# State-space turns of a two-block transformer kernel: seven GpSimd operations in place of five VectorE operations

## The reference, cut to what matters

```python
dt = jnp.exp(log_step.astype(f32))[:, None]
mag = jnp.exp(lr * dt)
ab_r = mag * jnp.cos(li * dt)
ab_i = mag * jnp.sin(li * dt)
...
_, _, s_r, s_i = lax.associative_scan(_complex_linear_combine, (a_r, a_i, bu_r, bu_i), axis=1)
```

## Time and profile before

| | |
|---|---|
| runs shown, median | 2434.28 us (3 runs, 2433.3 to 2437.17) |
| profiled execution, its own time | 2435.06 us |
| its span | 2433.4 us |
| granted TensorE clock over the span | 0.997 of full |
| PE busy | 2404.1 us |
| DVE, ACT, POOL busy | 1712.9, 1223.4, 527.3 us |

### The profile page before, as it was taken

The page is one execution under the profiler, slowest core; times in us unless marked ns, Lnnn a source line. Parts: engine busy times, 40 slices in busy tenths (PEclk is TensorE's granted clock), DMA queues, the critical chain, the costliest instruction groups (busy, mean ns, idle before and its releaser), DMA issues.

```text
span 2433.4 us, 45170 instructions
## 1 busy us (share of the span) xinstructions
PE 2404.1 (99%) x15288; PEld 2173.7 (89%) x15288; DVE 1712.9 (70%) x2649; ACT 1223.4 (50%) x1838; POOL 527.3 (22%) x1003
## 2 busy tenths in 40 slices
PE   8999999999999999999999999999999999999999
PEld 7888888989999999999999999998888888888888
DVE  8977776668888887678888875666555555555555
ACT  5455454455666665566665444444444444444442
POOL 2310032246767773210011221111000000000000
PEclk9999999999999999999999999999999999999999
DMA  7765566656666665555557876766777677777774
GB/s 243 218 201 198 189 216 209 188 184 202 198 204 209 200 196 179 187 185 196 167 189 245 262 219 223 228 201 179 204 191 191 191 192 190 190 190 192 190 190 147
DMA packets 257100, 485.07 MB, mean 199 GB/s; under 512 B 23688, under 2 KB 171860, under 8 KB 256736
## 3 DMA queue, kind: packets, MB, share of 16 engines
q1 hardware_dynamic: 216064, 415.66, 56.2%
q10 hardware_dynamic: 29632, 35.30, 4.5%
q0 software_dynamic: 11296, 32.68, 4.4%
HBM read 455.20 MB, written 31.08 MB: 200 GB/s over the span
## 4 chain that ended last, share of the span: by engine, by line
PE 85%; DVE 8%; issue 3%; ACT 3%; DMA 0%; ACTq 0%; DVEq 0%; SPq 0%; POOL 0%; POOLq 0%
PE z_ps L2191 14%; PE z_ps L2179 9%; PE z_ps L2181 9%; PE z_ps L2180 9%; PE z_ps L2192 7%; PE z_ps L2590 7%; PE z_ps L2591 7%; PE z_ps L2596 7%; DVE w_lo L1393 3%; ACT w_hi L753 1%; PE o_ps L2234 1%; PE s_ps L2216 1%; PE p_ps L2626 1%; PE o_ps L2626 1%; PE v_ps L2626 1%
## 5 line engine op out<-in xcount | busy, mean ns | idle before, releaser
L1393 DVE TENSOR_TENSOR w_lo<-w_raw,w_hi 128x1024 fp32r<-128x1024 f32 x518 | 638.9, 1262 | 221.4 <-ACT w_hi L753 219.5
L753 ACT ACTIVATE w_hi<-w_raw 128x1024 fp32r<-128x1024 f32 x518 | 529.4, 1050 | 243.1 <-PE z_ps L2192 130.3
L2050 DVE TENSOR_TENSOR w_lo<-w_raw,w_hi 128x1024 fp32r<-128x1024 f32 x262 | 320.8, 1226 | 300.5 <-ACT w_hi L1233 300.2
L2191 PE MATMUL z_ps<-x_both,w_hi 128*128 128x512 f32 x1440 | 517.9, 402 | 6.7 <-DVE w_lo L1393 3.5
L1233 ACT ACTIVATE w_hi<-w_raw 128x1024 fp32r<-128x1024 f32 x262 | 277.9, 1061 | 415.3 <-PE z_ps L2596 267.8
L2179 PE MATMUL z_ps<-x_both,w_hi 128*128 128x256 f32 x1376 | 398.5, 290 | 7.2 <-DVE w_lo L1393 6.5
L2192 PE MATMUL z_ps<-x_both,w_lo 128*128 128x256 f32 x1440 | 404.1, 281 | 0.0
L2181 PE MATMUL z_ps<-x_both,w_lo 128*128 128x256 f32 x1376 | 390.5, 284 | 0.0
L2180 PE MATMUL z_ps<-x_both,w_hi 128*128 128x256 f32 x1376 | 390.4, 284 | 0.0
L2191 PEld LDWEIGHTS z_ps<-x_both,w_hi 128*128 128x128 f32 x1440 | 271.8, 189 | 70.5 <-issue 7.1
L2179 PEld LDWEIGHTS z_ps<-x_both,w_hi 128*128 128x128 f32 x1376 | 265.0, 193 | 11.8 <-issue 10.1
(11 more groups left out here) (464 smaller groups left out, 4183.9 us busy)
## 6 DMA issues: line engine op xcount, KB each, us to landing
w_raw<-in_w SPq DMA_DIRECT2D x624, 512.0 KB, 4.3
w_raw<-in_w SPq DMA_DIRECT2D x160, 256.0 KB, 3.3
w_raw<-in_w SPq DMA_DIRECT2D x80, 384.0 KB, 4.9
w_raw<-in_w SPq DMA_DIRECT2D x80, 128.0 KB, 3.0
tab_d<-arena ACTq DMA_DIRECT2D x32, 256.0 KB, 2.9
res<-tab_d POOLq DMA_DIRECT2D x16, 384.0 KB, 5.6
arena<-tab_d POOLq DMA_DIRECT2D x16, 384.0 KB, 5.8
tab_d<-arena ACTq DMA_DIRECT2D x32, 128.0 KB, 2.5
```

The costliest lines, as they stand in the source:

```text
L753: act.activation(w_hi[:, n % RING, :], w_raw[:, n % RING, :], ACT.Copy).then_inc(w_hi_ready, 1)
L1393: dve.tensor_tensor(w_lo[:, n % RING, :], w_raw[:, n % RING, :], w_hi[:, n % RING, :].bitcast(F32), ALU.subtract).then_inc(w_lo_ready, 1)
L2050: dve.tensor_tensor(w_lo[:, k % RING, :], w_raw[:, k % RING, :], w_hi[:, k % RING, :].bitcast(F32), ALU.subtract).then_inc(w_lo_ready, 1)
L2191: pe.matmul(z[:], wh, both[:, :, kt, :], start=(first and kt == kts[0]), stop=False)
```

## The change

The turns of all 32 tiles are made on GpSimd. The bounded, reduced product is the same. VectorE has an operation that takes two tensors and a scalar at once, and it used that twice; on GpSimd each of the two is written as two operations, so the five become seven, with a wait on `turn_step` in front of each of the last four. The place changes too. VectorE made the even tile's turns behind the evacuation of the gate and the odd tile's ahead of the split for job 3 of the period. GpSimd makes them inside `tile_powers(st)`, behind the second of the three products of the loop, so ahead of the third and the last one. Tile 0's turns come behind the sums of squares of layer 0, behind a wait for the copy of `d_col` on VectorE, which reads a part of the same memory. The first wait of `tile_turns`, for `tab_ready`, goes along with it.

```diff
+            def tile_turns(st):
+                reach(pool, tab_ready, st)
+                f, f_hi, f_lo = (ssm_f[:, i, st:st + 1] for i in range(3))
+                pool.tensor_scalar(turn_k, times_in, f, ROUND, ALU.mult, ALU.add)
+                pool.tensor_scalar(turn_d, times_in, f_hi, None, ALU.mult)
+                pool.tensor_scalar(turns, times_in, f_lo, None, ALU.mult).then_inc(turn_step, 1)
+                pool.wait_ge(turn_step, 4 * st + 2)
+                pool.tensor_scalar(turn_k, turn_k, -ROUND, None, ALU.add).then_inc(turn_step, 1)
+                pool.wait_ge(turn_step, 4 * st + 3)
+                pool.tensor_tensor(turn_d, turn_k, turn_d, ALU.subtract).then_inc(turn_step, 1)
+                pool.wait_ge(turn_step, 4 * st + 4)
+                pool.tensor_tensor(turns, turns, turn_d, ALU.subtract).then_inc(turn_step, 1)
+                pool.wait_ge(turn_step, 4 * st + 5)
+                pool.tensor_scalar(turns, turns, 0.5, -0.5, ALU.min, ALU.max).then_inc(turns_ready, 1)
...
                 for m in range(3):
                     times(x[:, :, m + 1:8 - m:6 - 2 * m, :], x[:, :, m:9 - m:8 - 2 * m, :], xt_t, l_r, l_i, 3 + 3 * m)
+                    if m == 1 and st > 0:
+                        tile_turns(st)
                 times(x[:, :, 4, :], x[:, :, 3, :], xt_t[:, :, 0, :], l_r, l_i, 12)
...
+            pool.wait_ge(t_vec_landed, 16)
+            pool.wait_ge(turn_step, 1)
+            tile_turns(0)
             for st in range(1, ST):
                 tile_powers(st)
...
-                dve.tensor_scalar(turn_k, times_in, f, ROUND, ALU.mult, ALU.add)
-                dve.tensor_scalar(turn_d, times_in, f_hi, None, ALU.mult).then_inc(turn_step, 1)
-                dve.wait_ge(turn_step, 3 * st + 1)
-                dve.scalar_tensor_tensor(out=turn_d, in0=turn_k, scalar=-ROUND, in1=turn_d,
-                                         op0=ALU.add, op1=ALU.subtract).then_inc(turn_step, 1)
-                dve.wait_ge(turn_step, 3 * st + 2)
-                dve.scalar_tensor_tensor(out=turns, in0=times_in, scalar=f_lo, in1=turn_d,
-                                         op0=ALU.mult, op1=ALU.subtract).then_inc(turn_step, 1)
-                dve.wait_ge(turn_step, 3 * st + 3)
-                dve.tensor_scalar(turns, turns, 0.5, -0.5, ALU.min, ALU.max).then_inc(turns_ready, 1)
...
-                if l == 1:
-                    tile_turns(2 * h)
...
-                if l == 1:
-                    tile_turns(2 * h + 1)
```

More of the change, by code:

```diff
@@ L579, in load_c @@
                 pool.dma_start(c_in, ap["ssm_c"][st]).then_inc(c_landed, 16)
+            times_in = t_vec.rearrange("p (k i) -> p k i", i=STEP)[:, :, 0]
+            def tile_turns(st):
[12 more added lines that the diff above has]
+                pool.tensor_scalar(turns, turns, 0.5, -0.5, ALU.min, ALU.max).then_inc(turns_ready, 1)
             XT_STEPS = 15
@@ L1620, in _ @@
                     dve.wait_ge(consts_landed, (7 + STEP) * 16)
-                    chain(dve.tensor_copy(d_col.rearrange("p (c s) -> p s c", s=SPC), d_in))
+                    dve.tensor_copy(d_col.rearrange("p (c s) -> p s c", s=SPC), d_in).then_inc(turn_step, 1)
+                    dve.wait_ge(turn_step, 1)
                     chain(dve.memset(tab_out[:, 2 * P:3 * P], 0.0))
```

## The result

| | before | after |
|---|---|---|
| median of the runs | 2434.99 us (4 runs, 2433.3 to 2437.17) | 2563.98 us (4 runs, 2563.81 to 2566.1) |
| profiled execution, its span | 2433.4 us | 2562.3 us |
| granted TensorE clock over the span | 0.997 | 0.976 |

A forecast was written before the change was run, and what follows sets the result against it. PE, busy 2404.1 of 2433.4 us, was taken to bound the kernel. 15 x (5.7 wait + 2.4 clock) - 2.5 = 119 us on the profiled 2435.06 gave 2554, median 2553 us; range 2495 to 2585.

The forecast's parts named there:

- turns, undisturbed: POOL's seven operations a tile in layer 1, priced at a same-shape product's row: 2.27 us, bounds 1.4 and 3.1.
- a pair of splits in the chain: DVE's pair of splits for job 3's successor falls into POOL's new chain and costs POOL about 1.9 us.
- chain on POOL: From ACT's line 806 to PE's release at odd tiles: turns, third and last products, releases, splits; 7.0 us.
- slack of PE behind line 806: Time from ACT's end of line 806 on the even tile to PE's odd tile: mean 1.28 us, least 0.53.
- wait of PE: PE waits for POOL at the odd tile in fifteen of sixteen periods: 7.0 - 1.28 = 5.7 us each.
- low clock behind it: After each PE wait the granted clock drops; priced at the middle of 3.1 and 1.6 us: 2.4 us.
- start of the layer, once: Shorter 4.40 us PE wait for a split in layer 1's second period, plus 0.5 us elsewhere: -2.5 us.
- the room is there as a sum: POOL in layer 1: 19.2 us busy plus 4.6 added makes 23.8 of a 26.67 us period.
- Undisturbed and full clock: Rival, 12%: POOL interleaves better with DVE's splits and the clock holds; odd-tile wait 3.8 us, +55 us, 2489.
- Dear operations: Rival, 8%: each new POOL operation takes some 0.77 us, turns 5.6 us, wait 9.0; +180 us, 2614.
- The turns fit: Rival, 7%: POOL's chain is shorter than the slack; gain only at the layer's start, -3 to -6 us, 2430.
- hidden altogether: Rival, 3%: the turns fit the slack, with nothing gained at the layer's start either; 2434 us.

The follow-up runs named there:

- the run with one in seven: Changed kernel with turns moved behind the powers' last product and six of the seven operations left out, only the clamp kept: 2431.1 us, 0.9983 of the kernel before.
- the load alone: Kernel before, VectorE still making the turns, plus the seven operations on GpSimd behind each tile's powers from tile 3, into unread memory: 2468.62 us, 1.014.
- two sets of turns: Changed kernel with three small tiles of their own for odd tiles from 3 on, so turns wait for the tile before the last: 2479.34 us, 1.0179.
- The wait alone: Kernel before with only POOL's wait for ACT added at the place of the new turns, VectorE still making them: 2495.66 us, 1.0249.

## Why the prediction was right, and where it was not

**The mechanism holds.** PE waits for POOL at the odd tile of fifteen periods, and not at the even one, once the layer is under way. POOL begins its chain when ACT is through with line 806, since the turns exist once. Two parts of the chain were tried alone: the wait (+60 us without any turns) and the work behind it (1.49 us for a product of 1.52). The third, DVE's splits, is read from two kinds of waits in one run (1.19 against 3.13 us).

**The terms.** As they were put and as they came:

| a period | predicted | measured |
|---|---|---|
| turns, undisturbed | 2.27 us | 2.94 us |
| a pair of splits in the chain | 1.9 | 1.76 |
| chain on POOL | 7.0 | 7.66 |
| slack of PE behind line 806 | 1.28 | 1.39 |
| wait of PE | 5.7 | 6.26 |
| low clock behind it | 2.4 | 35.01 - 26.67 - 6.26 = 2.08 |
| start of the layer, once | -2.5 | +3.8 |

The pair is the mean length of the fifteen blocks of turns in the chain, 4.70 us, less 2.94. The last two rows are what is left over, of a period and of the 128.9 us, so that 15 x (6.26 + 2.08) + 3.8 = 128.9 comes out by itself. Independent readings stand beside them: 2.13 us a wait by the granted clock, 30.8 us more busy time of PE, and at the start PE ready for tile 3 at 580.32 - 6.15 = 574.17 us, 4.05 later than in the kernel before, which began it at 570.12. The forecast's sum was 9.9 us short: 8.4 by the waits and 6.3 by the start of the layer, less 4.8 by a clock term that was too dear. Part of the agreement is thus luck. So is the clock term itself, the middle of two gaps: the windows behind such waits spread from 0.58 to 0.80, and the shorter waits of the run with the turns one product later lost more. The bounds of the range had slips of 0.2 us, too: with turns of 1.4 us the chain adds up to 6.1 and not 5.9 (a wait of 4.8, not 4.6), and with 3.1 it is 7.8 without any further disturbance.

The turns were priced at the row of a product of the same shape, 0.29 us. The sums (lines 593 and 595) take 0.32 and the last operation 0.24, but lines 587 and 591 take 0.38 and the two reads of the times at lines 588 and 589 take 0.51 and 0.53. The input of lines 587 to 589 lies strided in `t_vec` (every fourth value), and a scalar comes from `ssm_f`. The stride alone is not what makes them dear: the one operation of the run with one in seven reads the same strided times with two constants and takes 0.295 us. Line 587, which reads both, takes 0.38. Why lines 588 and 589 take more stays open.

At the start of the layer the prediction named the risk and then booked the gain. In the changed kernel POOL's turns of tile 0 stand ahead of the powers of tile 1 and wait for DVE's copy:

```profile
523.49 0.38 POOL L587 TENSOR_SCALAR arena<-arena,ssm_f 128x64 f32<-128x64 f32 x1 [2.52 <-DVE ssm_em L1623]
523.85 2.53 POOL L588 TENSOR_SCALAR arena<-arena,ssm_f 128x64 f32<-128x64 f32 x1
...
530.31 0.29 POOL L616 TENSOR_TENSOR arena<-arena,ssm_c 128x64 f32<-128x64 f32 x1
```

The turns of tile 0 take 6.8 us, since four splits of DVE fall on them, and the powers of tile 1 start at 530.31 where they started at 521.30. PE waits 7.36 us at 544.32 in place of the 4.40 us before the split. With 1.58 us more at tile 2, the layer is some 4 us late where 2.5 us of gain were booked.

That the low clock follows from the gap is shown by the filler matmuls: with the gap filled to 0.97 to 2.21 us the clock stays at 1.00, and 2.0 us a period come back.

**What the prediction had wrong, though it cost it nothing.** It said that the room is there as a sum, 19.2 + 4.6 = 23.8 us of 26.67. The room is not there. Busy time leaves out what lies between one operation on POOL and the next that depends on it, which no other work fills. What POOL has to spare is what it waits for other engines, and one row of the waits of the kernel before has it, from 584.2 to 930.9 us:

```profile
POOL arena L598 <- DMA tab_d<-arena: 71.4, 13, 7.9
```

That is 71.4 / 13 = 5.5 us a period. Two blocks of turns are 2 x 2.94 = 5.9 without any disturbance, and they meet DVE's splits as well. So POOL is full, and from there on it sets the period: +34 us by the load alone, +39 to +41 with the turns behind the last product, +7 with half of them, and 4 us of gain with one operation of the seven. With room as the sum had it, the kernels with the turns behind the last product should have come out at 2434 to 2442 us; the two of them took 2476 and 2475, and the one with two sets of turns 2479.

This second cost does not show in the changed kernel. The wait for ACT makes its period 35 us long, and in 35 us POOL has room again: it waits 118.7 us for ACT. The costs do not add either. The wait alone is worth 60 us, the load alone 34, both together 129, because the seven operations stand in the chain behind the wait, where each of their microseconds is one of PE's.

**The rivals.** *Undisturbed and full clock* is excluded by the clock of 0.90. *Dear operations* had 0.77 us for each; the dearest undisturbed one took 0.53. *The turns fit* and *hidden altogether* fall with the waits. With hardly any load on POOL and the wait behind the last product, a gain of 4 us does exist, at the start of the layer, where that rival had it; but that kernel leaves the turns unmade. No full version tried beat the kernel before.

## What to carry to other kernels

Before work is moved to an idle engine, ask what it has to wait for there and what stands behind it in that engine's order: a small tile that exists once turns a loose sequence into a ring, and everything from the wait to the hand-over then counts in full. Read the room of an engine from its waits for other engines, not from its busy share: GpSimd was busy 72% of the stage and had 5.5 us of 26.67 to give. A gap on TensorE can be worth more than its length: the fifteen of 6.26 us cost a third more by the low clock behind them, while six of 1.19 to 3.13 us in the run with the wait alone had a clock of 1.00 behind them.

## What was not expected of the hardware

- The seven operations of 128x64 on GpSimd do not have one price. Undisturbed, a `tensor_scalar` with a strided input and a scalar from memory takes 0.38 us (line 587) to 0.53 us (line 589), one with contiguous input and constants 0.24 (line 597) or 0.38 (line 591), and a two-input operation 0.32. The Trainium skill (GPSIMD Engine Reference, Engine selection) has GpSimd about twice as slow as VectorE with two inputs and at roughly line rate with one. At this size these runs do not show it: VectorE's operations on two tensors took 0.32 and 0.33 us, as long as GpSimd's, and five of the seven have one input and are not the cheap ones as a group.
- A single operation of 0.5 us on GpSimd took 2.53 us at 523.85, and two of 0.32 took 1.12 and 1.18 us at 854.70, while VectorE ran splits. The loss is not fixed per operation.
- The loss to the low clock did not grow with the gap: 2.62 us behind waits of 4.77 us in the mean, 2.13 behind waits of 6.26.
- Forty matmuls in each gap, more work for TensorE, made the kernel 30.4 us faster than the same kernel without them.
